# Token products of the first layer's experts in column groups of 32 in place of 64

## The reference

```python
def ec_moe(h, w_r, w1, w3, w2):
    B, n, D = h.shape
    cap = max(1, EC_CAPACITY * n // N_EXPERTS)       # 2 * n // 16
    aff = jax.nn.softmax((h @ w_r).astype(jnp.float32), axis=-1)
    gate, idx = lax.top_k(jnp.swapaxes(aff, 1, 2), cap)
    xin = jax.vmap(lambda hb, ib: hb[ib])(h, idx)
    hid = jax.nn.silu(jnp.einsum('becd,edf->becf', xin, w1)) * jnp.einsum('becd,edf->becf', xin, w3)
    ye = jnp.einsum('becf,efd->becd', hid, w2) * gate[..., None].astype(h.dtype)
    return ...   # ye added into the chosen rows
```

## Time and profile before

| | |
|---|---|
| median of three runs | 4200.55 us |
| profiled execution: span, first to last instruction | 4194.4 us |
| TensorE busy in it | 3953.8 us (94%) |
| weight loads (PEld), beside it | 2671.2 us (64%) |
| DVE, ACT, POOL busy | 1686.9, 1022.7, 823.4 us |
| moved by DMA | 673.83 MB, mean 161 GB/s |
| first layer's expert stage | 2413.6 to 2958.8 us |
| second layer's expert stage | from 3713.9 us |

### The profile page before, as it was taken

One profiled execution on the slowest core, in us unless ns is written; L12 is line 12 of the kernel. 1 busy time (PEld: TensorE's weight loads), 2 busy tenths in 40 slices (PEclk: granted clock), 3 DMA queues, 4 the chain that ended last, 5 costly groups with the idle time before them and its releaser, 6 DMA issues. The chain is left out here.

```text
span 4194.4 us, 65008 instructions
## 1 busy us (share of the span) xinstructions
PE 3953.8 (94%) x28126; PEld 2671.2 (64%) x28126; DVE 1686.9 (40%) x2730; ACT 1022.7 (24%) x2127; POOL 823.4 (20%) x658
## 2 busy tenths in 40 slices
PE   8999999999999999998999799999899999979888
PEld 6788889887888766566555443333575778823332
DVE  2685854374445342637434300000435464421102
ACT  2212522222111131515211321111314252221111
POOL 2100022113452032212233101000222134400000
PEclk9999999999999999999999899999999999989999
DMA  3684300123223222010112399999320102389997
GB/s 113 212 282 148 90 18 4 45 95 118 81 81 103 68 62 71 23 61 1 61 61 100 128 382 394 393 394 367 112 88 26 61 21 101 121 355 427 427 427 307
DMA packets 196792, 673.83 MB, mean 161 GB/s; under 512 B 12174, under 2 KB 78414, under 8 KB 171678
## 3 DMA queue, kind: packets, MB, share of 16 engines
q1 hardware_dynamic: 190782, 649.76, 41.0%
q0 software_dynamic: 5728, 19.93, 1.6%
HBM read 647.50 MB, written 25.98 MB: 161 GB/s over the span
## 5 line engine op out<-in xcount | busy, mean ns | idle before, releaser
L559 PE MATMUL psum<-arena 128*128 128x264 f32 (+2 forms) x7120 | 1784.6, 413 | 16.5 <-DVE arena L627 6.5
L559 PEld LDWEIGHTS psum<-arena 128*128 128x128 f32 x7120 | 1350.1, 190 | 444.8 <-issue 11.7
L1458 PE MATMUL psum<-arena 128*64 128x512 f32 x3072 | 695.9, 599 | 43.2 <-DMA arena<-in_w_e 39.6
L1458 PEld LDWEIGHTS psum<-arena 128*64 128x64 f32 x3072 | 211.4, 137 | 464.7 <-issue 423.2
L594 ACT ACTIVATE arena<-psum 128x256 f32<-128x256 f32 (+2 forms) x405 | 169.8, 419 | 928.8 <-PE psum L559 871.1
L458 POOL TENSOR_TENSOR arena<-arena 128x512 f32<-128x512 f32 (+1 forms) x114 | 160.4, 1407 | 1027.2 <-PE psum L559 971.2
L2408 DVE TENSOR_TENSOR arena<-arena,psum 128x512 f32<-128x512 f32 x32 | 22.0, 688 | 765.1 <-PE psum L1468 509.8
L386 PE MATMUL psum<-arena 128*128 128x265 f32 (+2 forms) x1120 | 256.1, 386 | 3.3 <-ACT arena L3125 3.3
L386 PEld LDWEIGHTS psum<-arena 128*128 128x128 f32 (+1 forms) x1120 | 208.7, 188 | 43.0 <-ACT arena L3125 3.7
L2875 PE MATMUL psum<-arena 64*64 64x64 f32 x7424 | 225.9, 219 | 8.5 <-issue 4.5
L2875 PEld LDWEIGHTS psum<-arena 64*64 64x64 f32 x7424 | 224.0, 135 | 11.6 <-issue 8.8
(11 more groups left out here) (408 smaller groups left out, 3889.3 us busy)
## 6 DMA issues: line engine op xcount, KB each, us to landing
arena<-in_w_e SPq DMA_DIRECT2D x192, 2048.0 KB, 13.0
arena<-in_w_in SPq DMA_DIRECT2D x38, 2048.0 KB, 8.0
arena<-in_w_ada SPq DMA_DIRECT2D x24, 2048.0 KB, 8.5
arena<-in_ffn_up SPq DMA_DIRECT2D x22, 1024.0 KB, 7.6
arena<-in_w_branch SPq DMA_DIRECT2D x6, 2048.0 KB, 7.8
arena<-in_ffn_down SPq DMA_DIRECT2D x8, 1408.0 KB, 8.2
arena<-in_w_in SPq DMA_DIRECT2D x16, 512.0 KB, 4.4
arena<-in_w_out SPq DMA_DIRECT2D x4, 2048.0 KB, 8.0
```

What stands on the lines that cost most here:

```text
L559: mm = pe.matmul(PS[:, bank, 0:cn], loaded, moved, start=fresh and k == 0, stop=k == h - 1, skip_group_check=not fresh)
L1458: mm = pe.matmul(PS[c * HD:c * HD + HD, b + (m > 0), :], x(kk), w[:, k, c * BW:c * BW + BW], start=(kk == 0), stop=(kk == KT - 1))
```

## The change

In the first layer the two token matmuls of a k become four. Each takes 32 of the 64 tokens and writes 32 PSUM partitions: c = 0 goes to partitions 0 and 32, c = 1 to 64 and 96, so that both groups of one c read the same 512 columns of the slab. Values and places of the output are as before. The second layer keeps the two matmuls. Nothing is moved, and no wait is added or taken away; `mm`, which raises `slab_used`, is the last context product in the first layer as before.

```diff
                     for c in range(2):
-                        mm = pe.matmul(PS[c * HD:c * HD + HD, b + (m > 0), :], x(kk), w[:, k, c * BW:c * BW + BW],
-                                       start=(kk == 0), stop=(kk == KT - 1))
+                        if last:
+                            mm = pe.matmul(PS[c * HD:c * HD + HD, b + (m > 0), :], x(kk), w[:, k, c * BW:c * BW + BW],
+                                           start=(kk == 0), stop=(kk == KT - 1))
+                        else:
+                            for a in range(0, HD, 32):
+                                r = c * HD + a
+                                pe.matmul(PS[r:r + 32, b + (m > 0), :], x(kk)[:, a:a + 32], w[:, k, c * BW:c * BW + BW],
+                                          start=(kk == 0), stop=(kk == KT - 1))
```

## The result

The changed kernel takes 4172.84 us (median of 4 runs, 4172.31 to 4176.14) against 4203.35 us for the kernel before in the same comparison (4200.51 to 4206.56). The ratio is 0.9935 with a 95% interval of 0.9924 to 0.9947, so 22 to 32 us less.

The account below looks back on a forecast made before the run. TensorE was taken to bound the first layer's expert stage, with DMA close behind. Seam savings of 11.9, 13.0 and 0.4 us sum to 25.3, taking the span from 4194.4 to 4169.1; adding 6.15 gives 4175.3 us, range 4171 to 4186.

Parts of the forecast that it names:

- The seams: First layer's expert stage: losses where token and context parts alternate, 0.29 us a half slab; removing them saves 25.3 us.
- the three terms of the sum: First layer's expert stage: token to context 11.9 us, context directly to token 13.0, tokens behind hidden-value turns 0.4.
- Rival 3: Token-context seams come from the change of moving length or access pattern, not group width: 4200.6 us, chance 0.06.
- The slot of four groups: First layer's token parts: four 32-column groups share a slot, still 0.429 us; at worst 329 us more.
- Rival 4: Every token part: groups sharing slab columns can't be fed together and slots split; 4504 us if fully, chance 0.06.
- rival 2: First layer's token slots: a price per group in every slot, 8 ns x 768, giving 4181.4 us; chance 0.06.
- Code fetch: First layer's expert stage: some 13 code packets more, 0.13% of DMA time, costed at nothing.
- Transfers: First layer's slabs: 3% free DMA time (16 us) plus 16.8 us lead cover 23.8 us; no cost.
- The worst end of 7.0 us: First layer's stage: TensorE's wait if no slab landed sooner than now, 23.8 - 16.8 us.
- The gain kept whole: After the first layer's expert stage: later loads move along with its end, so all 25.3 us stay.
- The weak term: Whole kernel: 6.15 us between profiled span (4194.4 us) and median (4200.55), left as it is.

Follow-up runs that it names:

- equal lengths: Kernel before, 64-wide token products moved in pieces of 256 columns like the context's (first k keeps 512): 4208.97 us, stage 546.91 us.
- the third undone: Changed kernel with the two 64-wide token matmuls back for the third matrix alone (m = 2): 4177.94 us, stage 529.00 us.
- the run with half of the context: Changed kernel with half of the first layer's context products left out (two k of four per half slab): 4152.26 us, stage 498.97 us.
- the run with alternating order: Kernel before, with the context part ahead of the tokens in every second half slab of the first layer: 4194.39 us, stage 535.42 us.
- three buffers: Changed kernel with 3 slab buffers in place of 6 in the first layer: 4201.32 us, stage 547.01 us.

## Why the prediction was right

- *The seams* were sized right: 25.3 us forecast for the stage, 25.34 measured. Nor did errors cancel: the three terms of the sum, 11.9, 13.0 and 0.4 us, come to 11.95, 12.97 and 0.42 from the starts of all records. The changed kernel itself, equal lengths and the third undone (529.0 forecast, 529.00 measured) fix the cause: a change of column groups from 64 to 32 or back costs that at both lengths, and between equal widths a change of length or bank costs nothing. Why TensorE takes that time at the change, no run shows. Rival 3 falls.
- *The slot of four groups* was the unknown with the wide bounds. Two groups that read the same slab columns at once cost nothing: 429 ns as before. Rival 4 falls, and rival 2 with it. The Trainium skill (TensorE: Matmul & The Clock Gate, "Measured speedup vs the span model") gives about 4 ns of span for each further tile of a packed group. A slot's own span does grow here, from 0.60 to 0.61 us for four groups in place of two, but the next slot starts 429 ns after it with either, so in this stream the growth does not add up.
- *Code fetch:* 12 packets more (50 for 38), 13 forecast, and TensorE has no idle time but the two waits above.
- *Transfers:* no wait for a slab, as forecast. That they had room was argued from 3% of idle DMA time and the lead. Counted from the stage's start, the slab of the earlier trace rows was used 24.2 us sooner; 18.8 of that is that it landed sooner, and 5.4 came out of its lead. So both terms were at work, but the DMA share was a poor measure of the room: it rose only from 0.97 to 0.98 while the rate went from 378 to 396 GB/s, and the run with half of the context reached 412. It held more closely than the forecast reckoned, since the steady rate is within 1% of the transfers' limit and without the lead most of the gain goes. The lead was 17 to 19 us early in the stage and between 10 and 16 later, not as low as the 5 that I allowed. The worst end of 7.0 us was reckoned from one slab's lead; the shortest in the kernel before was 14.2 us.
- *The gain kept whole:* the span fell by 24.0 us, the stage by 25.3. The difference lies outside the stage. The stage began 3.9 us later; 3.4 of these arose in a stretch long before it (780 to 940 us), where the granted clock was 0.98 for 1.00, in code that the change doesn't touch. Behind the stage the two executions differ by 2.7 us the other way.
- *The weak term* is what lies around the span. I added 6.15 us, the distance of the profiled span to the median. The changed kernel's profiled execution took 4172.42 us with a span of 4170.4, so only 2.0 us lie around it, and seven runs of the kernel before in a later comparison lie 1.8 to 2.5 us above their spans. So the other 4 us were most likely an execution faster than the median of its kernel; its own time is not on record. The forecast of 4175.3 is 2.5 us above the measured median, and with 2.0 in place of 6.15 it would have been 1.7 below. Either is within the scatter of the runs, so that the total came so close is in part luck; the stage is what was forecast well. As a difference of medians the gain is 30.5 us, as a ratio 27 with 22 to 32, and 25.3 is within that.
- *A reading of the clock:* I called it close to full in every slice. Two slices of the earlier trace rows stand below 0.9. One is just ahead of the stage, where the granted clock is 0.50 from 2393.1 to 2413.5 us:

```profile
2393.10:2413.50 20.40, 5.66 (x24) 4.94 (x24) 7.27 (x27) 4.85 (x17) 7.19 (x10) 0.50 0.54 202
```

TensorE was busy for 5.66 of these 20.40 us. In both kernels the clock was full for the stage (1.00 in the earlier trace rows and in the stage's row after), so the forecast didn't suffer; in the run with alternating order it came back only some 3.5 us into the stage.

No run did better than the changed kernel while computing everything.

## What to carry to other kernels

Where short products of different column-group widths alternate on TensorE, count the seams: some 0.1 us at each change and a longer first slot after it, here 0.29 us in 5.45. Cutting the wider product to the narrower one's groups removed them at no price per slot here, with all four groups filled and the moving length kept. Before taking such a gain, look at how long ahead of its use a transfer lands, and at the rate that the transfers reach when TensorE no longer holds them back: a DMA share of 0.97 hid 5% of room in the steady rate (5.67 us a slab for 5.37), and the change took nearly all of it.

## What the runs showed of the hardware that was not expected

The loss at a seam is the same for token parts with a moving length of 512 and of 256 (0.100 us from 64 to 32 columns, 0.113 back), which I had expected; the first slot behind it had no expectation. It is 0.05 us longer at both lengths if the groups are 64 wide, but only 0.024 if they are 32 wide (0.45 for 0.43, 0.24 for 0.216). Two column groups may read the same columns of the moving operand in one slot without loss. And the busy share of the DMA engines hardly tells how much more they can move: 0.97 at 378 GB/s, 0.98 at 396, 1.01 at 412, and with three buffers in the changed kernel 0.99 at 387.
